# Products of zeros in a routing stage: shorter moving operands, and float32 on column tiles

## The reference

```python
def moe_swiglu(h, w_router, w_gate, w_up, w_down):
    t = h.reshape(-1, dm)
    logits = (t @ w_router).astype(jnp.float32)          # 256 x 8
    top_v, top_i = lax.top_k(logits, TOP_K)              # TOP_K = 2
    gates = jax.nn.softmax(top_v, axis=-1)
    comb = jnp.sum(jax.nn.one_hot(top_i, N_EXPERTS) * gates[..., None], axis=1)
    for e in range(N_EXPERTS):
        out = out + comb[:, e:e + 1] * swiglu(t, w_gate[e], w_up[e], w_down[e])
```

## Time and profile before

| | |
|---|---|
| Time, median of 3 runs | 1705.3 us (1704.7 to 1706.35) |
| Profiled execution, first to last instruction | 1705.2 us |
| TensorE busy | 1625.6 us, 95% |
| VectorE busy | 1271.7 us, 75% |
| ScalarE busy | 1041.4 us, 61% |
| Mean granted TensorE clock | 0.987 of 2.4 GHz |
| Read from memory | 441.66 MB |

### The profile page before, as it was taken

The page is one execution under the profiler, slowest core; times in us unless marked ns, Lnnn a source line. Parts: engine busy times, 40 slices in busy tenths (PEclk is TensorE's granted clock), DMA queues, the critical chain, the costliest instruction groups (busy, mean ns, idle before and its releaser), DMA issues.

```text
span 1705.2 us, 23552 instructions
## 1 busy us (share of the span) xinstructions
PE 1625.6 (95%) x9115; PEld 1364.1 (80%) x9115; DVE 1271.7 (75%) x1142; ACT 1041.4 (61%) x1034; POOL 194.8 (11%) x152
## 2 busy tenths in 40 slices
PE   8799999998999988989999999999999999999996
PEld 7679999877878767778888888888888888888884
DVE  5644444485847564678888888888888888888886
ACT  5453443554546453367777777777777777777773
POOL 0100000124423333010101001001001001010100
PEclk9799999999999999999999999999999999999999
DMA  9146555542222100589999999999999999999992
GB/s 349 58 141 210 176 191 177 173 138 91 69 100 75 50 1 2 221 292 405 373 373 378 381 383 375 376 379 371 378 378 374 367 388 369 378 375 379 378 404 103
DMA packets 158991, 450.97 MB, mean 264 GB/s; under 512 B 9648, under 2 KB 40784, under 8 KB 158928
## 3 DMA queue, kind: packets, MB, share of 16 engines
q1 hardware_dynamic: 155392, 436.96, 69.5%
q0 software_dynamic: 3536, 13.11, 2.0%
HBM read 441.66 MB, written 8.39 MB: 264 GB/s over the span
## 4 chain that ended last, share of the span: by engine, by line
PE 86%; DVE 7%; ACT 3%; issue 1%; SPq 1%; POOL 1%; DMA 1%; DVEq 0%; POOLq 0%; ACTq 0%
PE bank L1433 26%; PE bank L1435 25%; PE bank L1434 25%; PE bank L1824 1%; PE bank L1935 1%; PE bank L1834 1%; ACT whi L584 1%; DVE wlo L927 1%; DMA par<-in_attn_sinks_dram 1%; DVE wlo L1240 1%; DVE TT L1198 1%; DVE cvall L1107 1%; PE bank L1816 1%; PE bank L1862 0%; PE bank L1841 0%
## 5 line engine op out<-in xcount | busy, mean ns | idle before, releaser
L1240 DVE TENSOR_TENSOR wlo<-raw,whi 128x2048 fp32r<-128x2048 f32 x336 | 766.9, 2290 | 110.1 <-ACT whi L815 107.5
L815 ACT CAST whi<-raw 128x2048 fp32r<-128x2048 f32 x336 | 643.4, 1915 | 250.8 <-PE bank L1435 247.7
L1433 PE MATMUL bank<-whi,xhi 128*128 128x512 f32 (+1 forms) x1584 | 575.9, 364 | 11.4 <-DVE wlo L1240 2.9
L1435 PE MATMUL bank<-whi,xlo 128*128 128x512 f32 (+1 forms) x1584 | 567.8, 358 | 0.0
L1434 PE MATMUL bank<-wlo,xhi 128*128 128x512 f32 (+1 forms) x1584 | 567.1, 358 | 0.0
L1433 PEld LDWEIGHTS bank<-whi,xhi 128*128 128x128 f32 x1584 | 300.0, 189 | 59.8 <-issue 4.8
L1435 PEld LDWEIGHTS bank<-whi,xlo 128*128 128x128 f32 x1584 | 300.1, 189 | 44.2
L1434 PEld LDWEIGHTS bank<-wlo,xhi 128*128 128x128 f32 x1584 | 300.3, 190 | 41.3
L927 DVE TENSOR_TENSOR wlo<-raw,whi 128x2048 fp32r<-128x2048 f32 x74 | 178.5, 2415 | 80.3 <-ACT whi L584 80.0
L1433 PE MATMUL bank<-whi,ehhi 128*128 128x512 f32 x448 | 178.9, 399 | 5.4 <-DVE wlo L1240 3.9
L1435 PE MATMUL bank<-whi,ehlo 128*128 128x512 f32 x448 | 177.4, 396 | 0.0
(11 more groups left out here) (304 smaller groups left out, 1546.3 us busy)
## 6 DMA issues: line engine op xcount, KB each, us to landing
raw<-in_moe_w_gate_dram SPq DMA_DIRECT2D x112, 1024.0 KB, 6.8
raw<-in_moe_w_up_dram SPq DMA_DIRECT2D x112, 1024.0 KB, 6.6
raw<-in_moe_w_down_dram SPq DMA_DIRECT2D x112, 1024.0 KB, 7.2
raw<-in_dn_w_in_dram SPq DMA_DIRECT2D x24, 1024.0 KB, 5.2
raw<-in_ffn_w_gate_dram SPq DMA_DIRECT2D x11, 1024.0 KB, 5.5
raw<-in_ffn_w_up_dram SPq DMA_DIRECT2D x11, 1024.0 KB, 6.1
raw<-in_ffn_w_down_dram SPq DMA_DIRECT2D x11, 1024.0 KB, 5.0
raw<-in_dn_w_o_dram SPq DMA_DIRECT2D x8, 1024.0 KB, 5.1
```

The costliest lines, as they stand in the source:

```text
L815: act.copy(slot(whi, n, SPLIT), slot(raw, n, RAW)).then_inc(hi_ready, 1)
L1240: dve.tensor_tensor(slot(wlo, n, SPLIT), slot(raw, n, RAW), slot(whi, n, SPLIT).bitcast(F32), ALU.subtract).then_inc(lo_ready, 1)
L1433: pe.matmul(ps, lhs_hi, wh, start=start, stop=False)
L1435: return pe.matmul(ps, lhs_lo, wh, start=False, stop=stop)
```

## The change

Four calls of `keep_clock` in the routing stretch are replaced. `keep_shaped` does products of the same zeros with fewer moving columns, `keep_tiles` does float32 products with 32 stationary columns each, whose outputs go to partitions 0, 32, 64 and 96 of the bank, that is to the four column tiles of the array. Nothing else is touched; the other calls of `keep_clock` stay.

```diff
+            def keep_shaped(count, o_, columns):
+                for _ in range(count):
+                    for c in columns:
+                        pe.matmul(o_[:, 0:c], spare[:, 0:P], spare[:, 0:c], start=True, stop=True)
+
+            def keep_tiles(rounds, o_):
+                zeros_ = spare[:, :].bitcast(F32)
+                for _ in range(rounds):
+                    for j in range(0, P, 32):
+                        pe.matmul(o_[j:j + 32, :], zeros_[:, j:j + 32], zeros_, start=True, stop=True)
...
             i.then_inc(sem("gates_psum"), 1)
-            keep_clock(13, bank[1])
+            keep_shaped(20, bank[1], (192, 96))
             pe.wait_ge(sem("masks_ready"), 1)
...
-            keep_clock(8, bank[1])
+            keep_tiles(2, bank[1])
             pe.wait_ge(sem("h2lo_ready"), TB)
...
             pick(0)
-            keep_clock(4, bank[1])
+            keep_shaped(8, bank[1], (96,))
             gather(0)
-            keep_clock(6, bank[1])
+            keep_shaped(16, bank[1], (128,))
             pe.wait_ge(sem("gxlo_ready"), 2)
```

## The result

The changed kernel took 1712.3 us (median of 4 runs, 1710.4 to 1713.3) against 1705.8 us (4 runs, 1704.7 to 1707.2): a ratio of 1.0037, interval 1.0021 to 1.0053. A second set gave 1711.8 against 1707.0 us, ratio 1.0029 (1.0015 to 1.0043). By the medians it is slower by 6.5 and 4.8 us. The forecast was 1711.3 us. The time came out; two of the steps that led to it did not. The profiled execution took 1712.5 us with a span of 1710.7, so 1.8 us lie around a span; the 1705.2 us of the trace before thus stand for an execution of about 1707.0 us and not, as the prediction had it, for the median.

A forecast was written before the change was run, and what follows sets the result against it. The prediction took TensorE's product of weights to bound the kernel, with no slack after the routing. 1705.3 + 1.5 (first group) + 4.5 (second group) = 1711.3 us, range 1706.5 to 1717.0 us.

The forecast's parts named there:

- The bound and the carry: Whole kernel: TensorE's product of weights sets the end, so whatever the routing stretch takes longer is carried to the end.
- The load's floor: Short products in the routing stretch: each costs its 128-column stationary load, 0.21 us at clock 0.50, 0.111 at 1.00.
- the third rival: Short float32r products pay four cycles a column: 1716.8 us with serial tiles, 1712 to 1714 with overlapping; chance 0.18.
- The clock rises when it did: First group, ahead of the masks' product: clock still rises at 710.45, pairs cost their load floor, +1.5 us.
- own +3.0 for this case: First group with every product at clock 0.50: 8.5 us against 5.5, so +3.0 us.
- the row at 652.4 us: Clock row ahead of the routing: 0.50 during 40 products of 64 and 128 columns, then 0.99; small work raised it.
- The fourth rival: Routing stretch: the clock does not rise, the picking starts after 728.9, total 1720 us or more; chance 0.05.
- Serial tiles: Second group, between masks' product and picking: sixteen float32 records one after another, 6.8 us, adding 4.5 us; chance 0.42.
- the second rival: Second group: the four tiles run at once and stay hidden, price 0, total 1706.8 us; chance 0.09.
- The third and fourth group: Products around and after the picking: 0.89 against 0.93 us and 1.78 against 1.36 us, costing nothing.

The follow-up runs named there:

- The experiment with 128 columns: Against the kernel before, the first group is 26 products of 128 columns for 13 of 512; time ratio 1.0009 (0.9995 to 1.0022).
- first group alone: Against the kernel before, only the first group changed: 20 pairs of 192 and 96 columns for 13 products of 512; ratio 1.0021 (1.0008 to 1.0034).
- the kernel with one tile: Against the kernel before, second group is eight float32 products of 32 stationary columns, all outputs on partitions 0 to 31; ratio 1.0026 (1.0011 to 1.0041).
- 26 x 256: Against the kernel before, the first group is 26 products of 256 columns for 13 of 512; ratio 0.9993 (0.9979 to 1.0007).
- float32 on four tiles: Against the kernel before, the first group is three rounds of float32 products on four column tiles for 13 of 512; ratio 0.9995 (0.9982 to 1.0009).
- the version with the shortest routing stretch: Against the kernel before, 6 products of 512 ahead of the masks' product and 6 behind it, for 13 and 8; ratio 0.9981 (0.9970 to 0.9991).

## Why the prediction was right and where it was wrong

**The bound and the carry: right for this pair.** What the routing stretch took longer was carried to the end: 975.4 and 975.5 us behind it. Over all traces that part is 973.5 to 976.1 us long, by whether the clock falls once more behind the routing, and the prediction had no term for that.

**The load's floor: right.** 0.213 us a short product at 0.50. At 1.00 it is (724.7 - 723.1)/14 = 0.114 us for 128 columns, 0.111 forecast. Four cycles a column, the third rival, is out: 192 and 96 columns would have taken 0.48 us a pair at the full clock, and 96 alone 0.16, but the eight of 96 start 0.10 us apart (721.5 to 722.2).

**"The clock rises when it did", the step of the first group: wrong.** The term was +1.5 us. The first group is 7.7 and 8.5 us long in the change's two profiles instead of 5.0, that is +2.8 and +3.6, because the short products did not bring the clock back. (The prediction's own +3.0 for this case took 5.5 us for the thirteen; they took 5.0.) The prediction saw the question and answered it by the row at 652.4 us, where 40 small products had preceded a rise. That row speaks of other products: L1816 and L1824 are float32 with 64 stationary columns and go to two column tiles (next paragraphs), and at 0.50 a float32 record's 128 columns alone take a quarter of 0.853 us, 0.213, where 128 columns of float32r take half of that. The experiment with 128 columns decides against it here. The fourth rival, a clock that stays low, was the right mechanism at the wrong price: it was worked out with serial tiles and no end. In fact the long products or the tiles behind the masks raised it.

How the loss splits can be estimated from two profiles with a fall inside the router: from the zeros on the first group alone costs 5.5 us, 26 x 128, at the low clock as long as the thirteen, 2.6. So some 2.6 us are the clock's and some 2.9 the floor's, which at 0.50 is 20 x 0.427 - 13 x 0.427 = 3.0.

**"Serial tiles", the step of the second group: wrong.** It was +4.5 us. The measured one is nothing at the full clock. At the low clock the four groups of four records take 4 x 0.853 = 3.4 us. In the change they outlast VectorE, and the picking comes (719.50 - 715.50) = 4.0 us after the masks' product instead of 2.7: +1.3 us, a price that the clock sets, not the tiles: with the eight long products in their place it comes 4.4 us after (716.62 - 712.23, first group alone). The row taken, L1768, told what one tile does, and the kernel with one tile repeats it at 4.7 us.

The prediction's reason for that choice, that no row of the trace before has another column tile and none shows two products at once, was a misreading. L1824 writes float32 products to partitions 0 to 63 and 64 to 127 of a bank in turn, and stands in the very stretch of 652.4 us that the prediction used for the clock:

```python
                                i = pe.matmul(bank[q][64 * b:64 * b + 64, h % 2 * P:(h % 2 + 1) * P],
                                              (Ec if lv < LEVELS - 1 else TT)[:, 4 * b + h, 0:64], ident, start=True, stop=True)
```

Its first two records in the 0.02 us from 652.69 us, and eight of them with the next group's start:

```profile
L1824 PE MATMUL bank<-tabs,Ec x2: 475/475/475, 652.7 to 652.7; 128*64 128x128 f32 x2
...
652.70 1.12 PE L1824 MATMUL bank<-tabs,Ec 128*64 128x128 f32 x8
653.60 0.64 PE L1816 MATMUL bank<-TT,Ac 128*64 128x64 f32 x8
```

Two records start within 0.02 us, and eight take 0.90 us, where one after the other at L1768's price they would take 8 x 0.213 = 1.7. So the trace before had the second rival in it, though with two tiles and not four.

Here a rule had said better: the Trainium skill, "TensorE: Matmul & The Clock Gate", section "Part 3: Packing small matmuls", lets products on different tiles run side by side. The trace agrees, four starts within 0.1 us.

**The third and fourth group: right**, nothing.

**The sum.** 1.5 + 4.5 = 6.0 us was forecast; the two profiles have 4.0 and 5.5 us from the zeros on, the medians 6.5 and 4.8. That the number was met is luck: a loss that does not exist (serial tiles) stood in for one that was set too low (the clock). Between the two, the second rival, tiles at once with the clock as before, gives 1706.8 us and is as wrong in time as it was right about the tiles.

## What to carry to other kernels

A product with 128 stationary columns cost at least its load here (0.213 us at 0.50, 0.11 at 1.00), so under 256 moving columns a shorter one was no cheaper; and TensorE was "busy" throughout in the groups that brought the clock back (13 x 512, 26 x 256, float32 on four tiles) and in those that did not (26 x 128, 20 x (192, 96)), so look at the row of the granted clock and not at the busy share. Put such work where no other engine waits for what stands behind it; the version with the shortest routing stretch had seven products fewer ahead of such a wait. And before you take a nearest row because a trace lacks an operation, look through the code for where it writes: the column tiles were there, under another line.

## What the runs showed of the hardware

Four float32 products of 32 stationary and 512 moving columns, each on partitions of its own, run in the time of one: starts within 0.1 us for four records, 1.9 us for sixteen at the full clock, where one tile needs 7.05. Two float32 products of 64 stationary columns on the two halves of a bank's partitions do the same in the trace before. Twelve products on four tiles brought the clock from 0.50 to 1.00 after 6.7 us, as thirteen full-width products did. 26 products of 256 columns did so too, 26 of 128 did not, though at 0.50 both stand 0.213 us apart and TensorE's busy share is full in both.
